# Second RMS norm of a two-layer encoder: factor and shift applied to rows by token, scaled chunks turned inside the output projection

## What is computed

```python
x = x + gate1 * merged                       # merged = (...) @ w_out
h2 = rms_norm(x, norm_ffn) * (1 + scale2) + shift2
x = x + gate2 * grouped_moe(h2, ...)         # 16 experts, 4 groups, top 2 of the best group
# grouped_moe: scores = sigmoid(t @ w_router); picks from scores + router_bias
#              for e: a = silu(t @ w_gate[e]) * (t @ w_up[e]); out += gate[:, e] * (a @ w_down[e])
```

## Time and profile before

| | us |
|---|---|
| runs | 1519.23, 1517.80, 1517.92 |
| median | 1517.92 |
| the profiled execution | 1517.92 |
| its span in the trace | 1516.1 |

### The profile page before, as it was taken

The page is one execution under the profiler, slowest core; times in us unless marked ns, Lnnn a source line. Parts: engine busy times, 40 slices in busy tenths (PEclk is TensorE's granted clock), DMA queues, the critical chain, the costliest instruction groups (busy, mean ns, idle before and its releaser), DMA issues. The chain is left out here.

```text
span 1516.1 us, 19625 instructions
## 1 busy us (share of the span) xinstructions
PE 1433.4 (95%) x6948; PEld 1105.1 (73%) x6948; DVE 1000.1 (66%) x1258; ACT 857.3 (57%) x1242; POOL 143.2 (9%) x140
## 2 busy tenths in 40 slices
PE   6999989999989999999889999999998999999996
PEld 3777558887768878887567765788776888777774
DVE  1574785334389888888565748633355988888874
ACT  4632685323258777777454338732325677777764
POOL 0100000000021223221000000000000212222210
PEclk8999999999999999999999999999999999999998
DMA  9721751113259999999843258111245699999944
GB/s 357 250 100 67 288 213 56 56 56 111 107 189 375 380 376 366 369 369 369 319 178 111 74 193 291 55 56 56 78 144 205 229 379 380 366 376 362 366 161 171
DMA packets 148393, 341.25 MB, mean 225 GB/s; under 512 B 8307, under 2 KB 10633, under 8 KB 148200
## 3 DMA queue, kind: packets, MB, share of 16 engines
q1 hardware_dynamic: 136880, 317.20, 57.3%
q0 software_dynamic: 10720, 22.91, 4.0%
q10 hardware_dynamic: 728, 0.28, 0.1%
HBM read 332.82 MB, written 24.12 MB: 235 GB/s over the span
## 5 line engine op out<-in xcount | busy, mean ns | idle before, releaser
L801 PE MATMUL bank<-x_hi,w_lo 128*128 128x512 f32 x608 | 242.8, 399 | 9.9 <-DVE x_lo L2204 4.3
L803 PE MATMUL bank<-x_hi,w_hi 128*128 128x512 f32 x608 | 237.5, 391 | 0.0
L802 PE MATMUL bank<-x_lo,w_hi 128*128 128x512 f32 x608 | 237.4, 390 | 0.0
L2404 DVE TENSOR_TENSOR w_lo<-ring,x_lo 128x2048 fp32r<-128x2048 f32 x92 | 209.4, 2290 | 33.4 <-ACT x_lo L1682 33.4
L1682 ACT CAST zone_r<-ring 128x2048 fp32r<-128x2048 f32 x92 | 175.1, 1921 | 61.1 <-DMA ring<-in_w_gate 45.1
L1682 ACT CAST x_lo<-ring 128x2048 fp32r<-128x2048 f32 x92 | 174.9, 1926 | 52.3 <-DMA ring<-in_w_gate 44.1
L1225 PE MATMUL bank<-w_lo,zone_r 128*128 128x512 f32 x384 | 156.4, 407 | 0.3 <-issue 0.3
L1869 DVE TENSOR_TENSOR w_lo<-ring,w_hi 128x1024 fp32r<-128x1024 f32 x84 | 102.2, 1221 | 76.8 <-ACT w_hi L1402 76.0
L801 PEld LDWEIGHTS bank<-x_hi,w_lo 128*128 128x128 f32 x608 | 114.4, 188 | 42.0 <-issue 10.0
L802 PEld LDWEIGHTS bank<-x_lo,w_hi 128*128 128x128 f32 x608 | 114.4, 188 | 26.0 <-issue 2.4
L803 PEld LDWEIGHTS bank<-x_hi,w_hi 128*128 128x128 f32 x608 | 114.3, 188 | 24.2
(11 more groups left out here) (326 smaller groups left out, 2831.3 us busy)
## 6 DMA issues: line engine op xcount, KB each, us to landing
ring<-in_w_gate SPq DMA_DIRECT2D x32, 2048.0 KB, 16.5
ring<-in_w_up SPq DMA_DIRECT2D x32, 2048.0 KB, 17.0
ring<-in_w_down SPq DMA_DIRECT2D x32, 2048.0 KB, 12.0
ring<-in_w_ada SPq DMA_DIRECT2D x24, 2048.0 KB, 12.3
ring<-in_w_in SPq DMA_DIRECT2D x16, 2048.0 KB, 8.3
ring<-in_w_out SPq DMA_DIRECT2D x4, 2048.0 KB, 8.0
zone<-y_by_choice SPq DMA_DIRECT2D x8, 1024.0 KB, 8.2
ring<-in_w_branch_a SPq DMA_DIRECT2D x2, 2048.0 KB, 9.1
```

The costliest lines, as they stand in the source:

```text
L801: mm(out, lo, x_first, start=start, stop=False)
L802: mm(out, hi, x_second, start=False, stop=False)
L803: return mm(out, hi, x_first, start=False, stop=stop)
L2404: v.tensor_tensor(w_low[EXPERT_SLOTS[par][k]][:, cols], ring[EXPERT_SLOTS[par][k]][:, cols], part_hi[buf].bitcast(F32), ALU.subtract)\
```

## The change

`norm_apply`, `norm_shift`, the diagonal and the spread matmul go. Instead each chunk is multiplied by its scale alone, `mT[:, c] = xT[:, c] * mul1`, by ACT for seven chunks while the output projection runs, and by DVE for the last. PE turns these scaled chunks into rows, the first four chunks between groups 5 and 6 of the output projection (`ROWS_AFTER`), the rest behind it. The norm's factor is a number for each token, so on rows by token it is a factor for each partition: DVE puts factor and shift on the upper 512 columns straight from PSUM, ACT copies the lower 512 out and POOL puts factor and shift on them in two ops for each of four row blocks. The shift by column comes to all partitions through DRAM (`shift_dram`, `shift_rows`). The router runs on scaled chunks; DVE multiplies the scores by the factor and adds the shift's share (`route_const`), which PE has summed over partitions ahead of the output projection. Squares go to two buffers of their own. 16 filler matmuls (`ROUTE_WARM`) stand behind the scores, and those of the old chain go. The first half of `first_gate_low` moves from DVE to POOL, behind the row stores.

```diff
@@ psum uses
+    yield "route_add", (1,)
     for j in range(KC):
         yield ("out", j), (4, 5, 6, 7)
-    yield "mean2", (3,)
-    yield "spread2", (2,)
-    yield "router", (0,)
-    yield "scores", (1,)
     for half in range(2):
         for t in range(TT):
-            yield ("rows", t, half), (4, 5, 6, 7)
+            yield ("rows", t, half), (t,)
+    yield "router", (4,)
+    yield "mean2", (5,)
+    yield "scores", (6,)
-SHIFT_ACT = (0, 2, 4, 5, 7)
+ROWS_AFTER = 5
+ROUTE_WARM = 16
@@ tensor
+                ps = take(layer_use, "route_add")
+                pe.wait_ge(S["route_ready"], 1)
+                done(layer_use, "route_add", mm(ps[:, 0:GROUPS * KC * NE], K("ones"),
+                                                route_a.rearrange("p g k e -> p (g k e)"), start=True, stop=True))
+                def turn_chunk(c):
+                    if c < KC - 1:
+                        pe.wait_ge(S["z_ready"], c + 1)
+                    else:
+                        pe.wait_ge(S["z_last"], 1)
+                    for t in range(TT):
+                        key = ("rows", t, c // 4)
+                        ps = take(layer_use, key) if c % 4 == 0 else bank[layer_use[key][0]]
+                        ins = nc.tensor.transpose(ps[:, c % 4 * P:(c % 4 + 1) * P], mT[:, c, t * P:(t + 1) * P], K("ident"))
+                        if c % 4 == 3:
+                            done(layer_use, key, ins)
                 for j in range(KC):
...
+                    if j == ROWS_AFTER:
+                        for c in range(4):
+                            turn_chunk(c)
                 before = pairs_until(pe, layer)
+                for k in range(4):
+                    route(k)
+                for c in range(4, KC - 1):
+                    turn_chunk(c)
                 ps = take(layer_use, "mean2")
-                keep_warm(ps, 5)
-                pe.wait_ge(S["sumsq_ready"], 1)
+                pe.wait_ge(S["sq_added"], KC - 2)
                 for t in range(TT):
-                    ins = mm(ps[:, t:t + 1], tmp[:, 0, t * P:(t + 1) * P], K("ones")[:, 0:1], start=True, stop=True)
+                    mm(ps[:, t:t + 1], tmp[:, 0, t * P:(t + 1) * P], K("ones")[:, 0:1], start=(t == 0), stop=False)
+                pe.wait_ge(S["sq_ready"], 2 * KC * min(layer, 1) + KC)
+                for t in range(TT):
+                    ins = mm(ps[:, t:t + 1], out_squares[:, (KC - 1) % 2, t * P:(t + 1) * P], K("ones")[:, 0:1],
+                             start=False, stop=(t == TT - 1))
                 done(layer_use, "mean2", ins)
+                turn_chunk(KC - 1)
+                for k in range(4, KC):
+                    ins = route(k)
                 done(layer_use, "router", ins)
...
+                pe.wait_ge(free[layer_use["mean2"][0]], layer_use["mean2"][1] + 1)
+                keep_warm(bank[layer_use["mean2"][0]], ROUTE_WARM)
...
-                pe.wait_ge(S["rows_ready"], 2 * TT)
+                pe.wait_ge(S["rows_ready"], TT)
+                pe.wait_ge(S["rows_pool"], TT)
@@ scalar
                 for c in range(KC):
-                    norm_square(use, "out", c, mT)
+                    if c == KC - 1:
+                        af(warm[:, 0:1], eps[:, 0:1], ACT.Sqrt)
+                    norm_square(use, c)
+                    if c < KC - 1:
+                        scaled(c)
+                    if c == ROWS_AFTER:
+                        rows_half(use)
...
-                first_gate_high(0)
-                norm_shift()
...
+                act.wait_ge(S["raw_ready"], 1)
+                af(sc[:, :, :], sc[:, :, :], ACT.Sigmoid).then_inc(S["score_ready"], 1)
+                first_gate_high(0)
                 first_gate_high(1)
@@ vector
-                norm_apply(own, wait_full(dve, use, "spread2"))
...
+                v.reciprocal(tok_rstd2, tok_root2).then_inc(S["tok_rstd"], 1)
+                dve.wait_ge(S["tok_rstd"], 1)
+                dve.wait_ge(shift_back, (layer + 1) * 16 * GROUPS)
+                for t in range(TT):
+                    ps = wait_full(dve, use, ("rows", t, 1))
+                    v.scalar_tensor_tensor(rows_tok[:, t, 512:D], ps[:, :], tok_rstd2[:, t:t + 1],
+                                           shift_rows[:, t // 2, 512:D], ALU.mult, ALU.add).then_inc(S["rows_ready"], 1)
+                ps = wait_full(dve, use, "scores")
+                own.step(v.tensor_tensor(sc[:, :, :], ps[:, 0:TT * NE].rearrange("p (t e) -> p t e", t=TT),
+                                         tok_rstd2.unsqueeze(2).to_broadcast([P, TT, NE]), ALU.mult))
+                own.last()
+                v.tensor_tensor(by_group, by_group, route_const[:, :, :].unsqueeze(2).to_broadcast([P, GROUPS, 2, NE]),
+                                ALU.add).then_inc(S["raw_ready"], 1)
-                first_gate_low(0)
...
+                dve.wait_ge(S["rows_pool"], TT)
                 count = rank[:, TT * NE:(TT + 1) * NE]
...
+                dve.wait_ge(part_lo_ready, earlier * 12 + 1)
                 first_gate_low(1)
@@ gpsimd
+                pool.wait_ge(S["mod_ready"], 2)
+                for g in range(GROUPS):
+                    pool.dma_start(shift_dram[g:g + 1, :].rearrange("o (c p) -> p (o c)", p=P),
+                                   mod[:, 3 * KC:4 * KC, g], allow_slow_non_contiguous=True).then_inc(shift_out, 16)
+                pool.wait_ge(shift_out, (layer + 1) * 16 * GROUPS)
+                pool.wait_ge(S["m_ready"], KC)
+                for g in range(GROUPS):
+                    pool.dma_start(shift_rows[:, g, :], shift_dram[g].partition_broadcast(P)).then_inc(shift_back, 16)
+                pool.wait_ge(S["rows_half"], TT)
+                pool.wait_ge(S["tok_rstd"], 1)
                 for t in range(TT):
-                    pool.wait_ge(S["rows_ready"], TT + t + 1)
+                    half = rows_tok[:, t, 0:512]
+                    nc.gpsimd.tensor_scalar(half, half, tok_rstd2[:, t:t + 1], None, ALU.mult).then_inc(S["rows_scaled"], 1)
+                    pool.wait_ge(S["rows_scaled"], t + 1)
+                    nc.gpsimd.tensor_tensor(half, half, shift_rows[:, t // 2, 0:512], ALU.add).then_inc(S["rows_pool"], 1)
+                for t in range(TT):
+                    pool.wait_ge(S["rows_pool"], t + 1)
+                    pool.wait_ge(S["rows_ready"], t + 1)
                     pool.dma_start(h2_dram[t * P:(t + 1) * P, :], rows_tok[:, t, :]).then_inc(h2_out, 16)
+                pool.wait_ge(part_hi_ready, earlier * 12 + 1)
+                nc.gpsimd.tensor_tensor(w_low[first_gate][:, 0:2048], ring[first_gate][:, 0:2048],
+                                        gate_hi_first[0].bitcast(F32), ALU.subtract).then_inc(part_lo_ready, 1)
```

More of the change, by code:

```diff
@@ L1386, in group_root, with norm_square, scaled, rows_half @@
                       layer_use, ("sumsq", g))
-            def norm_square(use, what, c, out):
-                b, n = use[(what, c)]
+            def norm_square(use, c):
+                b, n = use[("out", c)]
                 act.wait_ge(free[b], n + 1)
-                af(out[:, c, :], xT[:, c, :], ACT.Square).then_inc(S["sq_ready"], 1)
+                if c >= 2:
+                    act.wait_ge(S["sq_added"], max(1, c - 2))
+                af(out_squares[:, c % 2, :], xT[:, c, :], ACT.Square).then_inc(S["sq_ready"], 1)
+            def scaled(c):
+                for g in range(GROUPS):
+                    tok = slice(g * SEQ, (g + 1) * SEQ)
+                    ins = af(mT[:, c, tok], xT[:, c, tok], ACT.Identity, scale=mul1[:, 1, c, g:g + 1])
+                ins.then_inc(S["z_ready"], 1)
+            def rows_half(use):
+                for t in range(TT):
+                    ps = wait_full(act, use, ("rows", t, 0))
+                    nc.scalar.copy(rows_tok[:, t, 0:512], ps[:, :]).then_inc(S["rows_half"], 1)
+                    act.wait_ge(S["rows_half"], t + 1)
+                    nc.scalar.sem_inc(free[use[("rows", t, 0)][0]], 1)
             def high_part(layer, n):
@@ L1849, in x_root_inverse, with add_square @@
                 v.reciprocal(x_rms[:, 0, :], x_rms[:, 1, :]).then_inc(x_rstd, 1)
-            def add_square(own, before, c):
+            def add_square(before, c):
                 if c == 0:
@@ L1855, in add_square @@
                 dve.wait_ge(S["sq_ready"], before + c + 1)
-                first = mT[:, 0, :] if c == 1 else tmp[:, 0, :]
                 if c > 1:
-                    own.last()
-                ins = v.tensor_tensor(tmp[:, 0, :], first, mT[:, c, :], ALU.add)
-                if c < KC - 1:
-                    own.step(ins)
-                else:
-                    ins.then_inc(S["sumsq_ready"], 1)
+                    dve.wait_ge(S["sq_added"], c - 1)
+                first = out_squares[:, 0, :] if c == 1 else tmp[:, 0, :]
+                v.tensor_tensor(tmp[:, 0, :], first, out_squares[:, c % 2, :], ALU.add).then_inc(S["sq_added"], 1)
             def low_part(n):
@@ L2234, in _ @@
```

(24 more changed lines are left out.)

115 lines of the change are left out of this document (47 added, 68 removed).

## The result

The changed kernel takes 1526.78 us, median of 14 runs, beside 1519.83 for the kernel before on the same chip: ratio 1.0051, 95% interval 1.0039 to 1.0063. Run again beside other kernels it took 1528.96 against 1519.59 (1.0057, 1.0041 to 1.0073). The forecast was no change, at 1518.0; it is 7 to 9 us slower. The profiled execution of after took 1532.03 us, its span is 1530.2; a second one had 1523.0.

The account below looks back on a forecast made before the run. The expert loop, bound by PE and DMA, passes on whatever the 36 us stretch ahead gives: 6.3 us a layer earlier, taken back by fillers and POOL holding DVE, net +0.1 a layer, so 1518 us from 1517.92, range 1508.5 to 1527.

Parts of the forecast that it names:

- rival C: Wait ahead of PE's row map: clock falls to about half, +3.5 us a layer, 1525 us; chance 0.22.
- T 2.07 us later, by the transposes: Output projection: 16 transposes moved between its groups 5 and 6 make its end come 2.07 us later.
- The route matmul: Ahead of the output projection's end: the shift's router matmul costs nothing, half a microsecond if PE's 1.64 us wait weren't there.
- First step on the scores at T + 10.15: First vector step on the scores 10.15 us behind the output projection's end, instead of 18.6; net 6.3 us a layer earlier.
- POOL holds DVE too, 4.4 us up to the picks: Scores to picks: each POOL op delays the DVE step behind it once; picks at 18.7 instead of 14.3 us.
- rival A: Behind the scores: DVE is never held by POOL, only fillers take time back, 1509.4 us; chance 0.24.
- B: Behind the scores: POOL holds DVE only in part, half the blocking, 2 us a layer gained, 1514 us; chance 0.16.
- The subtraction, 3.4 us: Behind the ranks: POOL's 128x2048 subtraction starts at 20.4, partly beside the place comparisons, and blocks L2351 until 23.8, 2.1 us.
- The fillers hide 2.1 us of the blocking: Ahead of the ranks: 16 fillers delay them 2.1 us anyway, so that much of POOL's 4.4 us blocking is hidden.
- The clock is kept: Own case, scores to first expert matmul: POOL and DVE hold each other, PE clock stays at 1.00; chance 0.38.
- The upper end of POOL's prices: POOL's ops behind the output projection at twice the lower end of 0.69 and 2.28 us: +4.2 us a layer, 1526 us.
- The estimate that I set beside the sum: POOL's ops at the skill's prices, 0.7, 1.2 and 4.5 us: +0.8 us a layer, 1519.6 us.

Follow-up runs that it names:

- experiment 1: Changed kernel with the small matmul of the shift's router share (route_add) on bank 3 instead of bank 1: 1527.22 us, ratio 1.0039 to the kernel before.
- experiment 8: Changed kernel, bank 3, POOL's arithmetic here on DVE, first gate's high and low parts moved into the wait for mean and root, fillers recounted: 1508.40 us, 0.9924.
- experiment 5: Kernel of Experiment 2 with POOL's second op of each pair given one input (factor added again, shift left out): 1515.03 us in one run.
- 6: Kernel of Experiment 2 with POOL's first op of each pair given two inputs (multiplied by the shift's row): 1521.12 us in one run.
- Experiment 2: Changed kernel with POOL's 128x2048 subtraction put on DVE, ahead of its wait for the ranks: 1520.26 us, ratio 1.0008 to the kernel before.
- experiment 3: Changed kernel with POOL's eight factor and shift ops on the lower half of the rows replaced by constant fills: 1518.21 us, ratio 0.9993 to the kernel before.
- experiment 9: Kernel of experiment 8 with one of four row parts back on POOL behind the reciprocal, and three bank increments moved: 1506.91 us, ratio 0.9912 to the kernel before.

## Why the prediction was wrong

Three steps failed: the matmul's bank, put at nothing; the hold of the subtraction, put too small and too late; and the clock, taken as kept. The direction of the loss was rival C's and its size too (1525 for 1526.8), but by another way than C's, so that C's number is met by luck. Step by step:

- **T 2.07 us later, by the transposes.** 1.80 us (46.36 with bank 3, 44.56 before). Right.
- **The route matmul "nothing, because PE waits 1.64 us behind it".** Wrong, the first failed step. The wait of the earlier trace rows stands at chunk 4 of the group, and the matmul was put at its head, in a bank whose last reader is DVE's last product with the gates, the very end of DVE's queue there. What I had read was that PE has time to spare in that neighbourhood, not what the instruction itself waits for. I bounded it at half a microsecond; it costs 0.8 to 3.6 us a layer, 1.8 on average, 0.8 of it the wait and the rest the clock behind it (experiment 1).
- **First step on the scores at T + 10.15.** 10.84 and 10.39, so 7.7 and 8.0 us earlier than before: the gain that the change was to bring is there. 0.7 us of b is register work ahead of the step, which I hadn't priced (experiment 8).
- **POOL holds DVE too, 4.4 us up to the picks.** 3.9 (8.00 less 4.11), so rival A is out. B's way, DVE getting in during a POOL op, exists, but only for ops with one input (experiment 5). That 4.4 is near 3.9 is luck, from two errors: POOL's ops are 1.57 and 1.28 us, not 1.0, which alone would have given more; but only those with two inputs hold, and three of them fall behind the scores (1.0 to 1.1 us each, and twice 0.4 beside one-input ops). The point that I left open, whether the second direction exists, is settled by experiments 2, 3 and 6.
- **The subtraction, 3.4 us, "blocks L2351 until 23.8, 2.1 us".** Wrong, and the largest term. It lasts 4.51 us, and it doesn't wait for the place comparisons: it catches the second L2374, 0.4 us behind the picks, at 438.73. My laying had POOL start at T + 20.4, and it did (439.91 is T + 20.4), but I let the ranks' step go first at 20.2. DVE stood from 438.73, 1.2 us ahead of POOL's row: by the start of the rows DVE came first, and it was held even so. The ranks' step came at T + 25.0 in layer 0. Against my laying the end of the plan is 32.7 instead of 29.95 behind T in layer 0, 2.8 us more, and 2.4 in layer 1. Experiment 2 takes 3.3 us back.
- **The fillers hide 2.1 us of the blocking.** They ended at T + 16.0 and the picks came at 18.8, which leaves PE the 2.98 us with nothing ahead of the ranks. My own numbers had this hole, 16.5 to 18.7; I counted it as time hidden, called it guarded under C, and did not ask what PE's standing still does to the clock.
- **The clock is kept (0.22 for C).** It falls: 0.50 from 440 us on. The hole isn't C's, ahead of the row map (there is none in after, since the slow first tile runs into it), but the two ahead of the ranks and of the first tile. Its price in f is 0.8 to 1.2 us a layer, a fourth to a third of C's 3.5.

Together, per layer, against the forecast's row: a +1.5 (by the mean over the layers with bank 1, 48.17), b +0.2 to +0.7, c -0.5, d and e +2.6, f +0.8 to +1.3, in all 4.6 to 5.6 us; a to f shows 5.8 and 5.2 more than forecast in the second execution, 7.4 and 5.5 in the first with its long a. For both layers that is 11 to 13 us, and the totals show 7 to 9; what lies between is within what the untouched stretches move from one execution to the next. The range ended at 1527, which holds the first median and not the second.

The upper end of POOL's prices gave 1526 in my own laying, and I had taken the middle for want of a row. That 1526 is near the result by luck as well, since it holds neither the bank nor the clock. The trace of before had none, but of the two ends the upper was the nearer to the chip: 1.57 and 1.28 are 2.3 and 1.9 times DVE's 0.69, 4.51 is 2.0 times 2.28. The estimate that I set beside the sum from the Trainium skill (GPSIMD Engine Reference, Performance versus the Vector engine), 4.5 us for the large one, is met by 4.51. Its word on one-input ops, "roughly line-rate" (the same page, Engine selection), isn't met: one input took 1.57 us where two took 1.27.

The Trainium skill's rule (SBUF — State Buffer, Who interferes with whom) lets the one who comes first have the pair for its whole instruction, and leaves out POOL instructions that only write SBUF. The runs agree for POOL's instructions with two SBUF inputs, if POOL is taken to come first ahead of its own row (last section), and for fills. They don't agree for those with one input: there DVE gets in after 0.4 us.

## What to carry over

An instruction moved to an idle engine is only free if that engine shares nothing with the busy one: POOL's elementwise work with two SBUF inputs took its whole length, twice DVE's own, out of DVE's two-input steps here, so a 2.3 us step given away cost 4.5. Put it where DVE reads PSUM, or keep it on DVE and look for a wait of DVE's to lay it in. And for every matmul that is put in, ask who reads its bank last, not whether PE has time nearby.

## What the runs showed of the hardware

- POOL's one-input 128x512 instruction takes 1.57 us, its two-input one 1.27, a 128x2048 with two inputs 4.51, a fill of 128x512 0.52.
- A one-input POOL instruction waits for a DVE subtraction with two inputs (3.1 us instead of 1.57, beside the 2.29 us subtraction, in both layers of experiment 5), but holds DVE by 0.3 to 0.4 us only. The two directions aren't alike. Why isn't known.
- The second instruction of L2374 has a row of its own in after's timeline:
```profile
438.73 5.78 DVE L2374 SCALAR_TENSOR_TENSOR zone<-zone 128x64 f32<-128x64 f32 x1
```
- DVE was held at 438.73, while POOL was still issuing its last row stores, 1.2 us ahead of the row of the subtraction that held it; layer 1 shows the same 1.2 us. In experiment 3, where POOL passed its last wait 0.7 and 0.6 us ahead of its subtraction (1.4 in after), DVE's long step starts 0.1 and 0.3 us ahead. What takes the hold that early stays open, it was not tried.
- After similar holes the clock did not fall each time: with the route matmul on bank 1 a stays at 47.15 in six layers and has 1.6 us more in seven. In experiment 9 PE has nothing for 0.57 us ahead of the row map in layer 0, and the clock is 1.00 until 438 and 0.50 from 440 on, behind the row map (f 5.13); in layer 1 it stays at 1.00 behind 0.58 us with nothing (4.11). In experiment 8 it is layer 1 that has the fall (5.34, 4.23 in layer 0).
